# Stacked high and low parts for the differential scores of seven heads, and a reordered turn of the keys

## What is computed

```python
q = rope(q, pos).reshape(B, S, DIFF_HEADS, 2, DIFF_QK_DIM)
k = rope(k, pos).reshape(B, S, DIFF_HEADS, 2, DIFF_QK_DIM)
def block(args):                       # 128 queries at a time
    s = jnp.einsum('bqhcd,bkhcd->bchqk', qblk, k).astype(jnp.float32) * scale
    s = jnp.where(kpos[None, :] <= qpos[:, None], s, -jnp.inf)
    p = jax.nn.softmax(s, axis=-1)
    a = p[:, 0] - lam * p[:, 1]
    return jnp.einsum('bhqk,bkhd->bqhd', a.astype(v.dtype), v)
o = rmsnorm(o, subln) * (1.0 - lambda_init)
y = o.reshape(B, S, DIFF_WIDTH) * jax.nn.silu(gate)
return y @ w_out
```

## Time and profile before

| | |
|---|---|
| timed runs | 2341.77, 2342.51, 2349.88 us; median 2342.51 us |
| profiled execution | 2343.61 us, its span 2341.8 us, so 1.8 us lie around the span |
| mean granted TensorE clock | 0.997 of full speed |
| busy share of the span | TensorE 98%, VectorE 62%, ScalarE 52%, GpSimd 51% |
| mean DMA traffic | 99 GB/s |

### The profile page before, as it was taken

One profiled execution on the slowest core, in us unless ns is written; L12 is line 12 of the kernel. 1 busy time (PEld: TensorE's weight loads), 2 busy tenths in 40 slices (PEclk: granted clock), 3 DMA queues, 4 the chain that ended last, 5 costly groups with the idle time before them and its releaser, 6 DMA issues.

```text
span 2341.8 us, 38883 instructions
## 1 busy us (share of the span) xinstructions
PE 2298.4 (98%) x13170; PEld 1907.6 (81%) x13170; DVE 1443.8 (62%) x2444; ACT 1209.4 (52%) x2606; POOL 1200.0 (51%) x834
## 2 busy tenths in 40 slices
PE   8999999999999999999999999999999999999998
PEld 7888888888877778778898988888766988988886
DVE  6554555554667776673454666787685514667686
ACT  5343344334655555654644754544576734645453
POOL 4443444442443334433662478786422842587885
PEclk9999999999999999999999999999999999999999
DMA  5333333332432222222531224232323431233332
GB/s 195 118 101 100 94 104 108 100 104 66 138 94 87 90 73 82 83 70 79 164 122 59 90 82 133 83 113 95 90 69 104 144 100 55 91 119 98 99 108 72
DMA packets 126554, 232.82 MB, mean 99 GB/s; under 512 B 17200, under 2 KB 17456, under 8 KB 126384
## 3 DMA queue, kind: packets, MB, share of 16 engines
q1 hardware_dynamic: 123536, 220.08, 30.1%
q10 hardware_dynamic: 2848, 10.49, 1.3%
HBM read 208.48 MB, written 2.10 MB: 90 GB/s over the span
## 4 chain that ended last, share of the span: by engine, by line
PE 63%; issue 18%; POOL 9%; DVE 5%; ACT 2%; DVEq 1%; ACTq 1%; DMA 0%; POOLq 0%
PE PS L605 55%; POOL wl L564 8%; PE PS L662 3%; PE PS L674 2%; POOL w L564 2%; PE PS L669 1%; PE PS L629 1%; DVE H L2120 1%; DVEq L2001 1%; DVE work L2153 0%; DVEq L2154 0%; DVE ul L2110 0%; ACT work L1381 0%; DMA raw<-tiles_dram 0%; DVE work L2034 0%
## 5 line engine op out<-in xcount | busy, mean ns | idle before, releaser
L564 POOL TENSOR_TENSOR wl<-raw,wh 128x512 fp32r<-128x512 f32 x502 | 718.9, 1457 | 847.6 <-ACT wh L1357 456.5
L605 PE MATMUL PS<-uh,wh 128*128 128x512 f32 (+1 forms) x2088 | 761.8, 365 | 2.4 <-DVE ul L2053 0.9
L605 PE MATMUL PS<-uh,wl 128*128 128x512 f32 (+1 forms) x2088 | 747.2, 358 | 0.0
L605 PE MATMUL PS<-ul,wh 128*128 128x512 f32 (+1 forms) x2088 | 746.5, 358 | 0.0
L605 PEld LDWEIGHTS PS<-uh,wh 128*128 128x128 f32 x2088 | 395.9, 190 | 78.3 <-issue 14.6
L605 PEld LDWEIGHTS PS<-uh,wl 128*128 128x128 f32 x2088 | 395.7, 190 | 58.4
L605 PEld LDWEIGHTS PS<-ul,wh 128*128 128x128 f32 x2088 | 396.2, 190 | 54.0 <-issue 0.5
L564 POOL TENSOR_TENSOR wl<-diagonals,wh 128x512 fp32r<-128x512 f32 x212 | 295.4, 1418 | 181.0 <-ACT wh L1357 141.1
L1521 ACT ACTIVATE work<-PS 128x512 f32<-128x512 f32 (+1 forms) x152 | 87.4, 575 | 350.6 <-PE PS L605 281.1
L605 PE MATMUL PS<-wh,forms 128*128 128x512 f32 x784 | 241.5, 389 | 0.0
L1357 ACT ACTIVATE wh<-raw 128x512 fp32r<-128x512 f32 x312 | 178.7, 622 | 95.9 <-PE PS L605 84.4
(11 more groups left out here) (271 smaller groups left out, 3467.8 us busy)
## 6 DMA issues: line engine op xcount, KB each, us to landing
raw<-tiles_dram SPq DMA_DIRECT2D x534, 256.0 KB, 2.8
diagonals<-tiles_dram SPq DMA_DIRECT2D x212, 256.0 KB, 3.0
work<-work SPq DMA_DIRECT2D x296, 64.0 KB, 2.0
gB<-post_dram ACTq DMA_DIRECT2D x8, 512.0 KB, 3.7
H<-x_dram SPq DMA_DIRECT2D x4, 512.0 KB, 5.8
H<-x_dram ACTq DMA_DIRECT2D x4, 512.0 KB, 5.2
work<-mem_dram ACTq DMA_DIRECT2D x2, 1024.0 KB, 6.7
out_dram<-H ACTq DMA_DIRECT2D x4, 512.0 KB, 2.7
```

What stands on the lines that cost most here:

```text
L564: nc.gpsimd.tensor_tensor(w_of(wl, slot)[:, hc], src[:, hc], w_of(wh, slot)[:, hc].bitcast(F32), ALU.subtract).then_inc(lo_ready, 1)
L605: last = nc.tensor.matmul(out, a, b, start=start and m == 0, stop=stop and m == 2, skip_group_check=goes_on)
```

## The change

**Scores.** Head 0 is scored as before, from buffers of its own (`first_q`, `first_k`). For heads 1 to 7 the turned queries and keys are split into an fp32r high part (ScalarE, `high_part`) and a low part (GpSimd, `low_part`, 128x512 each); SP then stacks them with DMAs (`stack_queries`: 4 of 64 partitions x 2 KB, `stack_keys`: 4 of 64 partitions x 4 KB), so that for each query-key pair the 128 partitions hold 64 rows of high and 64 of low parts of the queries, and for the keys once the high part in both halves and once the low part in both halves. A pair's scores are then two fp32r matmuls of 128 rows that accumulate, so four per block instead of two f32 matmuls of 64 rows.

**Order.** ScalarE makes the high part of the queries ahead of its split at j = 2, and of the keys behind its copy of block 1. GpSimd makes the low part of the queries ahead of the rest at j = 2 and of the keys ahead of the rest at j = 3. SP issues the stacking DMAs ahead of the third and the fourth load. On VectorE the turn of the keys moves from the end of the stage to behind the maximum of block 1, and the weights of block 1 lie between its cosine and its sine half; the maximum of block 3 stands alone at the end. TensorE waits for both stacks ahead of block 0 of each head.

```diff
--- before.py
+++ after.py
@@ -111,12 +111,16 @@
         colv = sb("colv", [P, NCOLS])
         rgw_sb = sb("rgw_sb", [P, 8, P])
         gB = sb("gB", [P, D])
+        with nc.sbuf_tensor("key_parts", [P, 2, S], F32R) as key_parts:
+            pass
         maskd = sb("maskd", [P, TT * 512], BF16)
         maskn = sb("maskn", [P, 768])
         stat = sb("stat", [P, 368])
 
 
         with nc.sbuf_tensor("work", [P, 16384], F32) as work:
+            pass
+        with nc.sbuf_tensor("work_parts", [P, 16384], F32R) as work_parts:
             pass
         forms = sb("forms", [P, 16, S], F32R)
         sb("work_rest", [P, 8192])
...
@@ -305,8 +313,11 @@
         dpt = H[:, :, :].rearrange("p n (h c) -> p n h c", h=2)
 
         def fraw(a): return wk(512 * (a % 2))
-        def fq(p): return wk(1024 + 512 * p)
-        def fk(p): return wk(2048 + 512 * p)
+        fq, fk = wk(1024), wk(1536)
+        first_q, first_k = wk(11264), wk(11776)
+        query_parts = work_parts[:, 2048:3072].rearrange("p (c n) -> p c n", c=2)
+        def query_stack(p, m): return w5[:, p, 512 * m:512 * m + 512]
+        def key_stack(p): return work_parts[:, 11264 + 2048 * p:13312 + 2048 * p].rearrange("p (m c n) -> p m c n", m=2, c=2)
         def fv(p): return wk(3072 + 512 * p).rearrange("p (t n) -> p t n", t=TT)
         fvt = wk(4096)
         def fgate(p): return wk(4608 + 512 * p)
@@ -513,12 +524,41 @@
                         swap_halves(draw(j), j, i * 10 + (j + 1))
             for n in range(N_D + 5, BASE["diff"] + 5):
                 load(n, n % 2)
-            with sp.Fori(0, HP) as i:
+            def stack_queries(p, parts):
+
+                sp.wait_ge(parts_lo, parts)
+                for m in range(2):
+                    for c in range(2):
+                        to = 64 * (m ^ c)
+                        sp.dma_start(query_stack(p, m)[to:to + 64, :].bitcast(F32),
+                                     query_parts[64 * m:64 * m + 64, c, :].bitcast(F32))\
+                            .then_inc(queries_stacked, 16)
+
+            def stack_keys(p, parts):
+
+                sp.wait_ge(parts_lo, parts)
+                for m in range(2):
+                    for to in (0, 64):
+                        sp.dma_start(key_stack(p)[to:to + 64, m, :, :].bitcast(F32),
+                                     key_parts[64 * m:64 * m + 64, :, :].bitcast(F32))\
+                            .then_inc(keys_stacked, 16)
+
+            def diff_loads(h, p, stacks=True):
+
                 for j in range(4):
-                    n = i * 4 + (BASE["diff"] + j + 5)
-                    load(n, (BASE["diff"] + j + 5) % 2)
+                    if stacks and j == 2:
+                        stack_queries(p, h * 2 - 1)
+                    if stacks and j == 3:
+                        stack_keys(p, h * 2)
+                    load(h * 4 + (BASE["diff"] + j + 5), (BASE["diff"] + j + 5) % 2)
                     if j < 2:
-                        swap_halves(fraw(j), j, i * 4 + (LIN["diff"] + j + 1))
+                        swap_halves(fraw(j), j, h * 4 + (LIN["diff"] + j + 1))
+
+            diff_loads(0, 0, stacks=False)
+            diff_loads(1, 1)
+            with sp.Fori(0, HP // 2 - 1) as i:
+                for p in range(2):
+                    diff_loads(i * 2 + (2 + p), p)
             def loads(first, end):
 
                 back = first - load_of(first)
@@ -583,7 +623,21 @@
                     rest(n, slot_of(n), form_source(n)[0])
 
             in_units = BASE["sw"] + 9
-            rests(N_D, BASE["x0"])
+            def low_part(parts, src, n):
+
+                pool.wait_ge(parts_hi, n)
+                nc.gpsimd.tensor_tensor(parts[:, 1, :], src, parts[:, 0, :].bitcast(F32), ALU.subtract).then_inc(parts_lo, 1)
+
+            d = BASE["diff"] + 4
+            rests(N_D, d + 3)
+            with pool.Fori(0, HP - 1) as i:
+                for j in range(4):
+                    if j == 2:
+                        low_part(query_parts, fq, i * 2 + 1)
+                    if j == 3:
+                        low_part(key_parts, fk, i * 2 + 2)
+                    rest(i * 4 + (d + 3 + j), slot_of(d + 3 + j), raw_of_tile(d + 3 + j))
+            rests(d + 3 + 4 * (HP - 1), BASE["x0"])
             rests(BASE["x0"], BASE["ff0"])
             ff_rests(0)
             rests(BASE["sw"], in_units)
@@ -921,9 +975,17 @@
 
             def diff_scores(A, p, u):
                 w = (u + 1) * P
+                if isinstance(A, int) and A == 0:
+                    scores(UNIT["diff"] + u,
+                           [(PS[:, SB0 + m, 0:w], first_q[64 * m:64 * m + 64, u * P:w],
+                             first_k[64 * m:64 * m + 64, 0:w], True, True) for m in range(2)])
+                    return
+                if u == 0:
+                    pe.wait_ge(queries_stacked, A * 64)
+                    pe.wait_ge(keys_stacked, A * 64)
                 scores(A * 4 + (UNIT["diff"] + u),
-                       [(PS[:, SB0 + m, 0:w], fq(p)[64 * m:64 * m + 64, u * P:w], fk(p)[64 * m:64 * m + 64, 0:w], True, True)
-                        for m in range(2)])
+                       [(PS[:, SB0 + m, 0:w], query_stack(p, m)[:, u * P:w], key_stack(p)[:, m, c, 0:w],
+                         c == 0, c == 1) for m in range(2) for c in range(2)])
 
             def diff_stage(L, A, par):
 
@@ -1624,6 +1686,11 @@
             def diff_pt(A, u):
                 pt(A * 4 + (UNIT["diff"] + u), fpt(u)[:, 0:(u + 1) * P], PS[:, TB0, 0:(u + 1) * P])
 
+            def high_part(parts, src, turned):
+
+                act.wait_ge(aux_taken, turned)
+                nc.scalar.activation(parts[:, 0, :], src, ACT.Copy).then_inc(parts_hi, 1)
+
             def diff_stage(L, A, par):
                 ap = 1 - par
                 former = A is not None and not (isinstance(A, int) and A == 0)
@@ -1634,6 +1701,8 @@
                         diff_exps(A - 1, par, 3)
                     n = L * 4 + (BASE["diff"] + j)
                     first = isinstance(L, int) and L == 0
+                    if j == 2 and not first:
+                        high_part(query_parts, fq, L * 3 + (AUX["diff"] + 1))
                     if not (first and j == 0):
                         split(n + 3, (slot_of(BASE["diff"]) + j + 3) % G_RING, (j + 3) % 2,
                               L * 2 + (BASE["diff"] // 2 + (j + 3) // 2 + 1), G_RING)
@@ -1653,6 +1722,8 @@
                         diff_pt(A - 1, 3)
                     if A is not None and j >= 1:
                         diff_pt(A, j - 1)
+                    if j == 2 and not first:
+                        high_part(key_parts, fk, L * 3 + (AUX["diff"] + 2))
                     if former and j == 1:
                         diff_squares(A - 1, par)
 
@@ -2364,8 +2435,9 @@
                                        ALU.mult, ALU.add)
                 v.drain().then_inc(probs_ready, 1)
 
-            def diff_rotate(L, a, par, between=None):
-                turn((fk if a else fq)(par), fraw(a), a, L * 4 + (LIN["diff"] + a + 1), L + 25, ftmp, between=between)
+            def diff_rotate(L, a, between=None):
+                to = (first_q, first_k) if isinstance(L, int) and L == 0 else (fq, fk)
+                turn(to[a], fraw(a), a, L * 4 + (LIN["diff"] + a + 1), L + 25, ftmp, between=between)
 
             def diff_values_in(A, p):
 
@@ -2384,10 +2456,11 @@
                     silu(fgate(ap), fgraw, fgexp, A * 4 + (LIN["diff"] + 4))
                     diff_max(A, 0)
                     diff_weights(A, ap, 0)
-                diff_rotate(L, 0, par)
+                diff_rotate(L, 0)
                 if A is not None:
                     diff_max(A, 1)
-                    diff_weights(A, ap, 1)
+                diff_rotate(L, 1, between=None if A is None else lambda: diff_weights(A, ap, 1))
+                if A is not None:
                     if former:
                         diff_norm(A - 1, par, between=lambda: diff_max(A, 2))
                     else:
@@ -2395,7 +2468,7 @@
                     diff_weights(A, ap, 2)
                     if former:
                         diff_scaled(A - 1, par)
-                diff_rotate(L, 1, par, between=None if A is None else lambda: last_max(L, A))
+                    last_max(L, A)
 
             def last_max(L, A):
```

More of the change, by code:

```diff
@@ L188, in build @@
         head_done = sem("head_done")
+        parts_hi = sem("parts_hi")
+        parts_lo = sem("parts_lo")
+        queries_stacked = sem("queries_stacked")
+        keys_stacked = sem("keys_stacked")
         act_step = sem("act_step")
```

## The result

| | before | after |
|---|---|---|
| timed runs, median (lowest to highest) | 2344.32 us (2341.77 to 2349.88, 6 runs) | 2361.19 us (2356.44 to 2366.32, 6 runs) |
| profiled execution, its span | 2343.61, 2341.8 us | 2356.44, 2354.6 us |
| mean granted TensorE clock | 0.997 | 0.994 |

The ratio is 1.0068, with a 95% interval of 1.0052 to 1.0084: the change costs 16.9 us by the medians. The profiled pair differs by 12.8 us; the profiled execution of the changed kernel was the fastest of its six.

What follows compares the result with a forecast made beforehand. TensorE, busy 98% of the span, was taken as the bound; block 2's weights had 0.8 us to spare. Six stages' +13.2 less 1.8 gave +11.4 us: 2355.0, by the median 2354; range 2333 to 2361.

Steps and rivals of the forecast that it cites:

- six stages at full clock: Stages 2 to 7, those with a norm: each 2.2 us longer because TensorE waits for block 2's weights, 13.2 us.
- head 7 at full clock: Head 7, scored behind the last stage without a key turn: 1.4 us saved plus a 0.4 us wait gone.
- falls of the clock: Rival: new 3.7 us gaps halve TensorE's clock, up to 3.7 us more each, three of six stages, 2365 us; chance 0.07.
- Who is late: At block 2's transposes, VectorE's weights drain at 786.5 instead of 783.0, so TensorE waits 3.7 us.
- The walk: VectorE's chain from key turn to block 2's weights, waiting out GpSimd instructions: 3.5 us later; total 2354 us, chance 0.50.
- The scores: Score matmuls on TensorE: a head falls from 3.75 to 2.35 us, saving 1.40 a head, 9.8 for seven.
- The step that failed is the straight line from 512 and 256 columns to 0.067 at 128: Block 0's scores: fp32r matmuls of 128 columns start 0.067 us apart, 0.27 us for the block.
- the estimate from the weight load: Block 0's scores: 107 ns per weight load holds each 128-column matmul, giving 0.43 us and 1.24 saved a head.
- The DMAs and ScalarE: Stacking loads, bounded at 2.8 to 11.2 us for landing, and ScalarE's two 0.58 us high parts: nothing added.
- the case that had 0.37: The whole run becomes slower by more than 0.5%, past 2354.2 us; chance 0.37.
- The signs: Confirming: four fp32r 128*128 records, 32.2 us stages, 3.7 us idle before block 2's transposes, four VectorE instructions over 1 us.
- four signs of being wrong: A 28.6 us stage without wait, a stack wait at L662, PEclk 0.5 in the stage, or over 0.1 us at 128 columns.

Runs made afterwards that it cites:

- the order alone: Kernel before the change with only VectorE's new order, f32 scores, no stacks or parts: 2341.23 us.
- norm early, high part late: Changed kernel, norm's first four small instructions ahead of block 1's weights, keys' high part made at j = 3: 2338.52 us, 0.9983 of the kernel before.
- low parts of 8 columns: Changed kernel with GpSimd's low parts of heads 2 to 7 made for only 8 of 512 columns: 2338.22 us.
- gap filled: Changed kernel with eight unused fp32r matmuls of 512 columns ahead of block 2's transposes in stages 2 to 7: 2352.02 us, 1.0034 of the kernel before.
- high part late: Changed kernel with ScalarE making the keys' high part at j = 3 instead of j = 2: 2351.23 us.
- norm early: Changed kernel with the norm's first four small instructions ahead of block 1's weights, keys' high part left in place: 2357.02 us, 1.0063 of the kernel before.
- low part twice: Changed kernel with GpSimd making the keys' low part twice, first into an unused tile: 2364.72 us.
- the run with 256 columns: Changed kernel with norm's start early and keys' high part at j = 3, block 0's score matmuls streaming 256 columns instead of 128: 2335.05 us.

## Why the prediction was right, and where it was not

**What the stages show together.** Stages without a fall of the clock, in the middle of the six, less the wait before the transposes of block 2 (which is up to 0.2 us shorter in the first and the last of the six):

| kernel | stage | wait | difference | falls in the six stages |
|---|---|---|---|---|
| before | 29.98 | 0 | 29.98 | 0 |
| the order alone | 30.50 | 0.44 | 30.06 | 0 |
| norm early, high part late | 29.44 | 0.56 | 28.88 | 0 |
| low parts of 8 columns | 30.03 | 1.15 | 28.88 | 0 |
| gap filled | 31.95 | 1.23 | 30.72, less 1.84 for eight matmuls at 0.23: 28.88 | 0 |
| high part late | 30.92 | 2.04 | 28.88 | 1 |
| norm early | 31.80 | 2.93 | 28.87 | 3 |
| after | 31.94 | 3.06 | 28.88 | 4 |
| low part twice | all with a fall: 34.34 | 3.82 | 30.52, less 1.64 for the fall: 28.88 | 6 |

The scores save 1.10 us a stage, in every kernel that has them in this form, and everything else is the wait and the clock.

**The sum, term by term** (profiled pair, us):

| term | forecast | measured |
|---|---|---|
| six stages at full clock | +13.2 | +11.2 |
| head 7 at full clock | -1.8 | -2.3 |
| falls of the clock | 0, a rival | +7.1 |
| sum | +11.4 | +15.9 |

The middle stages are 31.94, the last 31.73; the first, 31.66, holds half a microsecond of work at half clock and would be 31.42: 190.9 in sum, 11.2 over 179.75. The falls are the rest of the 196.98, 6.1, and 1.0 in head 7 (15.91 against 14.87 where the gap was filled).

- *Who is late:* right. The one wait that grew stands before the transposes of block 2, in the six stages with a norm; it was forecast at 3.7 us and measured at 3.06 or 3.07 in four of them. The low parts' removal and their doubling move it as a theory of turns wants, down to 1.15 and up to 3.82.
- *The walk:* right in each meeting. The sine product, the subtraction, L2387 and L2077 each waited out one of GpSimd's, and the weights' last instruction met a rest again. From block 3 to the end of L2077 it had 26.74 us (781.0 - 754.26), measured were 26.17; from there to the transposes 5.5, measured 5.46. Its hand-overs were each rounded up a little; the spread of 1.95 to 2.7 a stage held the 1.96. The Trainium skill ("SBUF — State Buffer", section "Who interferes with whom") names the shared port pair as an exclusive lock, held for a whole instruction; the rows agree, down to instructions of four columns, each 1.05 us or more where it takes 0.17 alone.
- *The scores:* forecast 1.40 saved, measured 1.10. From the transposes to the second matmul behind the scores, block 1 took 1.17 us before (769.98 to 771.15) and 0.82 after (744.43 to 745.25), 0.35 saved as forecast, and block 2 saves 0.33. Block 0 took 1.35 before and 1.12 after (737.16 to 738.28): 0.23 saved. The trace of before, from the transposes on:

```profile
762.49 0.66 PE L669 MATMUL PS<-cst,work 128*128 128x128 f32 x4
...
763.84 0.39 PE L605 MATMUL PS<-ul,wh 128*128 128x512 f32 x1
```

**The step that failed is the straight line from 512 and 256 columns to 0.067 at 128.** Its four matmuls take 0.48 (737.51 to 737.99), 0.12 each, as at 256 columns; the estimate from the weight load, 0.43, was the better one. That is 0.21 more than forecast, of which 0.12 is missing from the saving; the step from the transposes to the scores is shorter than before (0.35 where it was 0.59) and gives the rest back. Block 3 saves 0.22, counted in the same way: its 1.01 (729.15 to 730.16) is 0.10 more than four steps of 0.227. So blocks 0 and 3 each account for about 0.12 of the 0.3 missing, and why block 3 is dearer was not tested.

- *The clock:* **the term that was mis-sized.** It stood among the rivals with a chance of 0.07 and a price of 3.7 us a time. It came behind four of the six waits: 2.8 us for the longer fall, 1.6 for each of the next two, 1.0 for the one in head 7, together 7.1 us, and the filled gap gave 9 back by the medians. So it came more often than was forecast and cost less each time: half of the 3.4 us at half speed is lost, not as much as the gap is long. The chance was too low because I used one row of a halved clock, with TensorE at work on little, and none of an idle gap. No stage of the kernel before has a gap of three microseconds, but the end of its trace has one that I overlooked: the last matmul ends at 2333.42, no other follows, and the clock falls 2.6 us later.

```profile
2335.00:2336.00 1.00, 0.00 (x0) 0.00 (x0) 1.00 (x1) 0.93 (x3) 0.00 (x0) 1.00 0.39 156
2336.00:2337.00 1.00, 0.00 (x0) 0.00 (x0) 0.45 (x3) 0.47 (x2) 0.00 (x0) 0.51 0.00 0
```

The Trainium skill ("TensorE: Matmul & The Clock Gate", section "Why this matters for your kernels") warned of idle gaps between bursts of matmuls, and the runs bear it out: the clock fell behind all six gaps of 3.8 us and behind four of the six of 3 us. As a rule that speaks against the change it deserved a third of the chances or more.

- *Head 7:* -1.8 forecast, -2.3 measured, -1.3 with its fall of the clock. 1.7 of it comes from VectorE's order, 0.6 from the scores, where I had 0.4 and 1.4. With the late high part of the keys head 7 takes 15.48, not 14.87; of the difference 0.45 is a wait of TensorE for VectorE behind block 3.
- *The DMAs and ScalarE:* nothing, as forecast. 4.4 us for the keys' stack lies between the bounds of 2.8 and 11.2, and nobody waits for it, even with the high part later.
- *The total:* 2361.19 lies 7 us above 2354 and at the upper end of the range from 2333 to 2361. Of the 7 us 1.8 are the base: the median of the kernel before is 2344.32 over six runs, and was 2342.51 over the three that the forecast had. In the rest errors of opposite sign meet: the six stages 2.0 too dear, head 7 0.5 too dear, the clock 7.1 too cheap. That the total lies no further off is luck in part: the upper end allowed for one or two falls at 3.7 us, and four came, which cost 7.1 together. The change is slower by more than the 0.5% that can be told from none, the case that had 0.37; most of the chances, 0.60, stood on a difference that can't be told.
- *The signs:* those for the walk came (four records, 31.94 where I had 32.2, the four VectorE instructions over 1 us). Of the four signs of being wrong two came as well: 0.5 in PEclk inside the stage, and 0.12 us from start to start at 128 columns.

What stays open: why a wait of 3.06 us is followed by a fall in some stages and not in others, and why one fall lasts twice as long. The 4 us between the profiled pair's difference and the medians' may come of falls that differ from execution to execution, as in the mixer; of the executions that were only timed there is no trace.

## What to carry to other kernels

Work put on an idle GpSimd is not free when VectorE has a chain with little slack: count each VectorE instruction with SBUF operands of four columns or more that stands beside it as one GpSimd instruction long (those of one column were not held up here), walk through the meetings, and move small VectorE instructions to where GpSimd idles (0.17 against 1.1 us here), looking at once for whom the displaced GpSimd work meets next. A new idle gap of some 3 us on TensorE cost more here than the gap; if the wait can't be removed, work in the gap can pay even when its result is thrown away. And an fp32r matmul of 128 columns was no cheaper here than one of 256.

## What the runs showed of the hardware that was not expected

- **The clock falls behind some idle gaps and not behind others.** By the last column of the table above, and the run with 256 columns: no fall behind gaps up to 1.25 us (30 gaps in five kernels, the filled one among them), 1 of 6 at 1.8 to 2.04 us, 3 of 6 at 2.8 to 2.9, 4 of 6 at 2.9 to 3.07, 6 of 6 at 3.7 to 3.8. A gap of 1.72 us ahead of the differential stages, near 609, is followed by a fall in two of the six profiles that have it (the late high part, the filled gap). In the stages a fall lasts 3.4 us, once 6.8. It can come while TensorE is still idle: in the changed kernel's first stage with a norm TensorE resumes at 694.10, and PEclk is down in the window before.

```profile
693.00:694.00 1.00, 0.00 (x0) 0.00 (x0) 0.92 (x1) 0.65 (x2) 1.00 (x2) 0.62 1.07 299
694.00:695.00 1.00, 0.91 (x4) 0.94 (x5) 0.96 (x3) 0.00 (x0) 1.00 (x1) 0.50 0.76 217
```

- **Idle work can be a gain.** 48 useless matmuls made the changed kernel 9 us faster.
- **Turns are waited out by tiny instructions too.** VectorE instructions of 128x4 with SBUF operands took 0.88 to 1.22 us when they began inside a GpSimd instruction, 0.16 or 0.17 otherwise. Those of 128x1 (L2428, L2432) took 0.16 and 0.28 beside a rest, and L2407, which reads PSUM, 1.36 for its four beside one and 1.37 without.
- **128 and 256 columns cost the same in fp32r** with 128 rows and columns of weights: 0.12 us from start to start.
